# One kernel of two transformer blocks: where the second block's filters are made

## The chip, the cores and the metric

The kernel runs on one core of one Trainium2 chip. The time is the device time of one launch in microseconds (us); of several runs the median counts. Beside the timed runs there is one execution taken by the hardware profiler, from which all rows below come.

The engines are PE (matrix products), DVE and POOL (elementwise work), ACT (elementwise work and functions from tables; a table has to be loaded before its functions can run), and SP, which only issues transfers (DMA) here. Each engine works through its own list of instructions in order and waits for others at semaphores.

## The reference

Block 1 is two layers, each a mixer (a gated recurrence beside an attention) and a feed-forward part: in layer 0 a dense one, in layer 1 a mixture of 8 experts of which each token takes 2. A norm ends it. Block 2 is again two layers, conditioned by a vector, on 256 tokens and 256 tokens of context. The mixer of its layer 0 has a hyena branch, whose filters depend on nothing but weights:

```
def hyena_filters(n, w1, b1, w2, b2, freq, w3):
    hdn = jnp.sin(fr * (z @ w1 + b1))            # z: 256 x 33, positions
    hdn = jnp.sin(fr * (hdn @ w2 + b2))          # 64 wide
    filt = hdn @ w3                              # 2 orders x 2 directions x 512
    return filt.reshape(n, 2, 2, 512) * decay[:, None, None, :]

def bidir_long_conv(z, h_fwd, h_bwd, d_skip):
    taps = concatenate([h_fwd, 0, h_bwd[:0:-1]])                 # 512 long
    taps = taps * rsqrt(sum(taps * taps, axis=0) + EPS)
    y = irfft(rfft(z, 2 * n) * rfft(taps))[:n]
    return y + z * d_skip

def modulated_norm(x, g, shift, scale):
    return rms_norm_2(x, g) * (1 + scale) + shift
...
x = first_block(...)            # ends in rms_norm(x, final_norm)
h = modulated_norm(x, ...); h_ctx = modulated_norm(ctx, ...)
p = h @ w_in; p_ctx = h_ctx @ w_in
```

All is fp32. So between the experts of block 1 and the first product of block 2 stand two norms of x one behind the other, and one of the context.

## The kernel before

**Weights.** They stream through as 496 panels of 1 MB (128 x 2048 fp32) into a ring of six places in SBUF. SP issues panel p when panel p - 5 has been multiplied (`load`, line 466; the loop of line 479 for the first 462 panels, then one by one). Panels 0 to 461 belong to block 1; of them the experts have 8 x 42, three of which are a step. Then come 13 panels of block 2's layer 0 (`project2`, two of 512 columns in each), 4 of its output, and the same for layer 1.

**Products.** A product in fp32 is made of three products of a faster form: each operand is cut into a high part (ACT, the names with `high`, line 1425) and the rest (DVE subtracts the high part from the whole; `ring_low`, line 2709, for a panel of block 2, `h_parts`, line 2641, for the activations). 48 such products are a panel. Small things, the filters among them, are multiplied in plain fp32. All matrix products carry line 513 in the profile, all of ACT's operations line 1425.

**The end of the experts.** The rows of the last expert are put back to their tokens by products with a 0/1 matrix (`scatter`; `G`, `rows_high`, `rows_low`) into PSUM, and DVE adds them to x, a quarter at a time (line 2477).

**The seam.** `hyena_filters`, once per engine, holds the two norms and the filters interwoven, in the order in which it is written:

- PE: the first hidden product, the mean squares of x, the second hidden product, the mean squares of the context, taps(0) (the four products of order 0 with w3: two halves of the positions, `tb`, by two directions, `d`), the mean squares of x once more, taps(1), energy(0), spectrum(0) (eight products of 512 columns with the dft tables), energy(1). Then panels 0 and 1, then `spectrum(1)`, then panel 2.
- DVE: the halvings of panels 1 and 0, between them and after them the eight operations that bring each hidden layer's argument into the range of the sine (lines 2566 to 2573), the reciprocal of the first norm and eight scalings of x (line 2608), taps(0) and taps(1) times decay (line 2580), the reciprocal of the two second norms (line 2615), `condition(0)` (line 2634), and the loop of 16 steps that makes h (line 2620) and 16 that make its low part (line 2641). After the loop the reciprocals of the filters' energies (2587) and the eight operations that normalise the spectra (2596, 2599).
- ACT: squares, roots, the two sines, and the high parts (`y_parts`) of h. The sine and the root lie in different tables.
- POOL: for either order the sum and the difference of the two directions' taps (lines 1980 and 1981).
- SP: the filters' eight tables and the context, issued behind panels 463 (lines 488 to 492) and 466 (494 to 497).

**Block 1's start.** ACT squares x, PE sums it (8 products), ACT takes the root, DVE the reciprocal; panel 0 follows.

Of the kernel before, what the change touches and what calls it, by code (L numbers as in the profile page):

```python
# [126 lines left out]
def dft_tables():  # L127

    t = np.arange(S, dtype=np.float64)
    a = np.pi * np.outer(t, 2 * t + 1) / 512.0  # L130
    rows = lambda m: m.reshape(2, P, S).transpose(1, 0, 2).reshape(P, 2 * S)
    return np.concatenate([rows(np.cos(a)), rows(np.sin(a)), rows(np.cos(a).T / 256), rows(np.sin(a).T / 256)],
                          1).astype(np.float32)


def decay_table():
    t = np.linspace(0.0, 1.0, S, dtype=np.float32)[:, None]
    deltas = np.linspace(np.log(1e-2) / 1.5, np.log(1e-2) / 0.3, 512, dtype=np.float32)
    d = np.exp(-t * np.abs(deltas)).astype(np.float32)
    return d.reshape(2, P, 512).transpose(1, 0, 2).reshape(P, 1024)  # L140


def position_table():
# [3 lines left out]
    return np.concatenate([t, np.cos(f * w), -np.sin(f * w)], -1).T.astype(np.float32)  # L147


def two_blocks(nc, panels, x_in, ctx_in, consts_in, small_in, dft_in, decay_in, pos_in, w1_in, w2_in, w3_in,  # L150
               skip_in, rpb_in, out):
    stack = ExitStack()
    with stack:
# [40 lines left out]
        rt = sb("rt", 400)  # L194
        zrow = sb("zrow", 640, dt=BF16)
# [127 lines left out]
        COMBINED = (6144, 4096)  # L323

        def rnorm(o):

            return proj[:, 2304:2816] if o else proj[:, 3456:3968]

# [132 lines left out]
        def _(sp):  # L464
# [14 lines left out]
            with sp.Fori(1, looped) as r:  # L479
                for s in range(RING):  # L480
                    sp.wait_ge(DONE, r * RING + (s - RING + 1))
                    load(r * RING + s, s)
            biases = [(h, r) for h in range(8) for r in range(4)]
            for p in range(looped * RING, PANELS):
                sp.wait_ge(DONE, p - RING + 1)
                load(p, p % RING)
                if p == BLOCK1 + 1:
                    sp.dma_start(proj[0:33, 2816:2880], w1_in).then_inc(sem("filter_entry_landed"), 16)
                    sp.dma_start(proj[0:33, 2048:2304], pos_in).then_inc(sem("filter_entry_landed"), 16)
                    sp.dma_start(proj[0:64, 2880:2944], w2_in).then_inc(sem("filter_entry_landed"), 16)  # L490
                    sp.dma_start(proj[0:64, 0:2048], w3_in).then_inc(sem("filter_tables_landed"), 16)
                    sp.dma_start(cT[:, :], ctx_in).then_inc(sem("context_landed"), 16)
                elif p == BLOCK1 + 4:
                    sp.dma_start(proj[:, 8192:9216], decay_in).then_inc(sem("filter_tables_landed"), 16)
                    sp.dma_start(arena[:, 8704:9728], skip_in.partition_broadcast(P)) \
                      .then_inc(sem("filter_tables_landed"), 16)
                    sp.dma_start(arena[:, 4096:6144], dft_in).then_inc(sem("filter_tables_landed"), 16)
# [11 lines left out]
        def _(pe):  # L509
# [253 lines left out]

            def every_expert(p0):
# [45 lines left out]
                down(p0 + E * FFN - 1, 1, 0, STEPS)  # L810

# [152 lines left out]
            def compact_experts(p0):  # L964

                def scatter(ex, js):
                    for j in js:
                        if 4 * ex + j > 1:
# [110 lines left out]
                last_down()  # L1079
                pe.wait_ge(sem("rows_split"), E)  # L1080
# [3 lines left out]

            accs = [1]
            pe.wait_ge(sem("early_landed"), 32)
            pe.wait_ge(sem("accumulators_free"), 1)
            for layer in range(2):
                for j in range(4):
                    mean_square(j, MEAN_BANK[0])  # L1090
                if layer == 0:
                    pe.wait_ge(sem("consts_landed"), 16)
                    project1(layer)
# [15 lines left out]
            def hyena_filters():  # L1109
                h1 = proj[0:64, 2304:2560]  # L1110
                h2 = proj[0:64, 2560:2816]

                def taps(o):
                    for tb in range(2):
                        for d in range(2):
                            last = mm(bank(4 + tb * 2 + d), h2[:, tb * P:(tb + 1) * P],
                                      proj[0:64, (o * 2 + d) * 512:(o * 2 + d + 1) * 512], True, True)
                    last.then_inc(sem("filter_taps_sum"), 1)

                def energy(o):  # L1120
                    pe.wait_ge(sem("taps_squared"), nth(pe, "taps_squared"))
                    if o:
# [1882 lines left out]
```

## Time and profile before

| | us |
|---|---|
| median of 3 runs | 2281.84 |
| lowest and highest | 2280.45, 2283.21 |
| the profiled execution | 2276.82 |
| its span in the trace | 2275.0 |
| PE, DVE, ACT, POOL busy in the span | 2184.2, 1266.8, 690.9, 13.1 |
| 16 DMA engines, mean rate over the span | 234 GB/s |

The start of a row is counted from the start of the span. A row's duration is that of one instruction, or, with "x8" at its end, of eight behind one another; a plain fp32 product counts as two records. In square brackets stands how long the engine had been idle before, and what ended that.

### The profile page before, as it was taken

To read this page: it belongs to the slowest core of one execution; us is meant where nothing else is said; L and a number is where in the kernel's file an instruction comes from. 1 tells how busy PE (TensorE), PEld (TensorE's weight loads), DVE (VectorE), ACT (ScalarE), POOL (GpSimd) and SP (SyncE) were. 2 spreads that over 40 slices of the span, in tenths; PEclk is the share of its full clock that TensorE was granted. 3 is DMA by queue.
4 is the path that set the end of the run, shared out by engine and by line. 5 is a ranking of instruction groups with operands and counts; after the bars stand their busy time and mean duration, and the time that the engine had idled before them with its cause. 6 is when DMAs were issued, how large, how long until landed. Compare 5 with 4: busy or idle time off the path is not lost.

```text
span 2275.0 us, 41269 instructions
## 1 busy us (share of the span) xinstructions
PE 2184.2 (96%) x17170; PEld 1414.0 (62%) x17176; DVE 1266.8 (56%) x2570; ACT 690.9 (30%) x893; POOL 13.1 (1%) x25
## 2 busy tenths in 40 slices
PE   8999999999999899999999999999989999898988
PEld 7899899999899633333333333333336784677856
DVE  5765544437855344444444454445467666847783
ACT  6464433337464200010001000100024222634452
POOL 0000000000000000000000000000001000000000
PEclk9999999999999899999999999999999999999999
DMA  6244577756234299999999999999991220016400
GB/s 261 107 144 147 199 269 271 262 192 223 109 131 150 110 390 397 387 383 380 409 388 371 388 403 390 381 381 403 387 360 37 74 97 33 1 56 136 109 16 20
DMA packets 81811, 532.03 MB, mean 234 GB/s; under 512 B 16935, under 2 KB 17224, under 8 KB 17480
## 3 DMA queue, kind: packets, MB, share of 16 engines
q1 hardware_dynamic: 81528, 528.95, 61.0%
q8 instruction: 110, 1.80, 0.3%
q10 hardware_dynamic: 144, 1.05, 0.1%
q14 instruction: 29, 0.24, 0.0%
HBM read 528.91 MB, written 1.05 MB: 233 GB/s over the span
## 4 chain that ended last, share of the span: by engine, by line
PE 78%; DVE 12%; ACT 6%; issue 3%; DMA 1%; DVEq 0%; ACTq 0%; SPq 0%
PE ps L513 77%; ACT arena L1425 2%; ACT B_high L1425 1%; DMA ring<-panels 1%; PE ps L1343 1%; ACT L1425 1%; DVE arena L2822 1%; DVE arena L2184 1%; DVE arena L2208 1%; DVE ring_low L2709 1%; DVE arena L2198 1%; DVE ring_low L2070 1%; ACT P_high L1425 1%; DVE arena L2179 0%; DVE hT L2035 0%
## 5 line engine op out<-in xcount | busy, mean ns | idle before, releaser
L513 PE MATMUL ps<-ring,arena 128*32 128x512 f32 (+1 forms) x3056 | 894.0, 566 | 2.7 <-DMA ring<-panels 1.4
L513 PE MATMUL ps<-ring,hT 128*32 128x512 f32 x5376 | 794.9, 593 | 0.0
L513 PEld LDWEIGHTS ps<-ring,arena 128*32 128x32 f32 x3056 | 231.5, 110 | 593.7 <-issue 543.5
L1425 ACT ACTIVATE arena<-ps 96x256 f32<-96x256 f32 (+3 forms) x199 | 93.9, 478 | 883.8 <-PE ps L513 862.7
L2440 DVE STREAM_TRANSPOSE arena<-arena 32x64 f32<-32x64 f32 x1344 | 316.0, 235 | 20.9
L2487 DVE SCALAR_TENSOR_TENSOR arena<-arena,rt,ps 96x256 f32<-96x256 f32 x112 | 53.4, 477 | 472.4 <-ACT arena L1425 472.4
L513 PEld LDWEIGHTS ps<-ring,hT 128*32 128x32 f32 x5376 | 213.0, 110 | 6.9 <-issue 6.7
L513 PE MATMUL ps<-h_parts,ring_low 128*128 128x256 f32 x704 | 200.0, 284 | 0.0
L513 PE MATMUL ps<-h_parts,B_high 128*128 128x256 f32 x1024 | 189.3, 287 | 1.9 <-DVE h_parts L2044 1.1
L513 PE MATMUL ps<-y_parts,ring_low 128*128 128x256 f32 (+1 forms) x512 | 173.0, 338 | 0.0
L513 PEld LDWEIGHTS ps<-h_parts,B_high 128*128 128x128 f32 x1024 | 161.3, 194 | 3.2 <-issue 2.0
L2300 DVE TENSOR_TENSOR W_low<-ring,W_high 128x2048 fp32r<-128x2048 f32 x42 | 96.2, 2292 | 116.8 <-ACT W_high L1425 116.8
L513 PEld LDWEIGHTS ps<-h_parts,ring_low 128*128 128x128 f32 x704 | 135.9, 193 | 0.0
L513 PE MATMUL ps<-h_high,W_high 128*128 128x256 f32 x448 | 129.0, 288 | 2.8 <-DVE h_low L2049 1.7
L513 PE MATMUL ps<-h_low,W_high 128*128 128x256 f32 x448 | 126.6, 283 | 0.0
L513 PE MATMUL ps<-h_high,W_low 128*128 128x256 f32 x448 | 126.6, 283 | 0.0
L2070 DVE TENSOR_TENSOR ring_low<-ring,B_high 128x2048 fp32r<-128x2048 f32 x40 | 91.2, 2291 | 62.3 <-ACT B_high L1425 61.7
L1425 ACT ACTIVATE W_high<-ring 128x2048 fp32r<-128x2048 f32 x42 | 80.3, 1912 | 93.9 <-DMA ring<-panels 49.0
L513 PEld LDWEIGHTS ps<-y_parts,ring_low 128*128 128x128 f32 x512 | 98.1, 192 | 10.2
L1425 ACT ACTIVATE proj<-ps 128x512 f32<-128x512 f32 (+2 forms) x86 | 65.1, 756 | 104.5 <-PE ps L513 103.8
L513 PEld LDWEIGHTS ps<-h_high,W_high 128*128 128x128 f32 x448 | 85.7, 191 | 11.0 <-issue 9.2
L513 PEld LDWEIGHTS ps<-h_low,W_high 128*128 128x128 f32 x448 | 85.8, 191 | 0.0
(281 smaller groups left out, 3367.7 us busy)
## 6 DMA issues: line engine op xcount, KB each, us to landing
ring<-panels SPq DMA_DIRECT2D x496, 1024.0 KB, 7.3
arena<-rpb SPq DMA_DIRECT2D x32, 64.0 KB, 8.4
cst<-consts SPq DMA_DIRECT2D x1, 1632.0 KB, 12.1
xT<-x SPq DMA_DIRECT2D x1, 1024.0 KB, 4.8
cT<-ctx SPq DMA_DIRECT2D x1, 1024.0 KB, 13.6
arena<-dft SPq DMA_DIRECT2D x1, 1024.0 KB, 19.6
y<-xT ACTq DMA_DIRECT2D x1, 1024.0 KB, 3.9
proj<-w SPq DMA_DIRECT2D x1, 512.0 KB, 12.0
```

The costliest lines, as they stand in the source:

```text
L513: return nc.tensor.matmul(o, w, m, start=start, stop=stop, skip_group_check=skip)
L1343: last = nc.tensor.transpose(bank(TURN_BANKS[layer] + half)[:, c * P:(c + 1) * P], probs(layer, i, half)[:, c * P:(c + 1) * P], K(K_ID))
L1425: return nc.scalar.activation(o, i, fn, **kw)
L2070: V.tensor_tensor(wide_low(q, 0, PW), ring[:, (q % RING) * PW:(q % RING + 1) * PW], proj_high(layer, i).bitcast(F32), ALU.subtract).then_i ...
L2184: signal(V.tensor_tensor(v(E[lv % 2]), v(b), v(b)[:, :, B - 1:B].to_broadcast([P, 512 // B, 2 * B]), ALU.subtract), "level_exponent_ready")
L2198: signal(V.tensor_tensor(w(X), qk, w(E[lv % 2]), ALU.mult), "level_qk_ready")
L2208: step(V.reciprocal(lf, lf))
L2300: V.tensor_tensor(split(W_low, q, 0, PW), ring[:, (p % RING) * PW:(p % RING + 1) * PW], split(W_high, q, 0, PW).bitcast(F32), ALU.subtract ...
L2440: last = V.transpose(hidden_T(s)[group(b), :, 32 * g:32 * g + 32], src[group(g), :, b, :])
L2487: V.scalar_tensor_tensor(hb[s % 2], sg[s % 2], slot_weight[0:SLOTS, ex:ex + 1], bank(s % 2)[0:SLOTS, 256:512], ALU.mult, ALU.mult) \
L2709: V.tensor_tensor(wide_low(q, 0, PW), ring[:, (q % RING) * PW:(q % RING + 1) * PW], N_high[p % 2].bitcast(F32), ALU.subtract).then_inc(sem ...
L2822: signal(V.tensor_scalar(pr, pr, stat_of(3, i, half), None, ALU.mult), "probs_ready")
```

## The change

- **The hidden layers** (two products, 2 x 8 operations on DVE, two sines) are made at the start of block 1: the first ahead of its first norm, the second in the first panels of layer 0. Their result stays in a tensor of its own, `filter_hidden`. Their small weights come on ACT's queue at the start.
- **The tables** come while the experts run: SP issues w3 and the context after round 65 of the ring, decay after round 68, the dft tables after round 71, skip behind panel 468.
- **The last expert.** PE multiplies half of taps(0) (`half_taps(0, 1, 2)`) between the last expert's last panel and the scatter; ACT squares the context there. Each quarter of x is signalled alone (`x_part`).
- **The norms** (`final_norms`) hold no more of the filters than the two halves of taps(0).
- **Between the panels** of layer 0 `filter_step(turn)` makes the rest: after panel 0 taps(1), after 1 spectrum(0), after 2 both energies (one product each, since POOL adds the squares up first), after 3 and within 4 spectrum(1).
- **Radix 2.** Positions and frequencies are ordered even and odd, so that a spectrum needs four products instead of eight and a butterfly. ACT copies the products out, POOL normalises, adds skip and makes the butterfly: 18 operations in place of 4. The hyena's transposes and its last products read and write in that order, with a stride.
- No code of block 2's layer 1 is changed, nor of block 1 beyond the hidden layers.

The diff, cut to its core:

```diff
 # SP
-            with sp.Fori(1, looped) as r:
-                for s in range(RING):
-                    sp.wait_ge(DONE, r * RING + (s - RING + 1))
-                    load(r * RING + s, s)
+            rounds(1, 66)
+            sp.dma_start(proj[0:64, 0:2048], w3_in).then_inc(sem("filter_tables_landed"), 16)
+            sp.dma_start(cT[:, :], ctx_in).then_inc(sem("context_landed"), 16)
+            rounds(66, 69)
+            sp.dma_start(proj[:, 8192:9216], decay_in).then_inc(sem("filter_tables_landed"), 16)
+            rounds(69, 72)
+            sp.dma_start(arena[:, 4096:6144], dft_in).then_inc(sem("filter_inputs_landed"), 16)
+            rounds(72, looped)
...
 # PE
+            def half_taps(o, tb, b):
...
+                for d in range(2):
+                    last = mm(bank(b + d), filter_hidden[0:64, tb * P:(tb + 1) * P],
+                              proj[0:64, (o * 2 + d) * 512:(o * 2 + d + 1) * 512], True, True)
...
                 last_down()
+                pe.wait_ge(sem("rows_c_copied"), E)
+                half_taps(0, 1, 2)
                 pe.wait_ge(sem("rows_split"), E)
                 scatter(E - 1, (0, 1))
...
+            pe.wait_ge(sem("filter_inputs_landed"), 48)
+            mm(bank(3)[0:64, 0:S], W1_T, POS_T, True, True).then_inc(sem("filter_products_done"), 1)
...
+            def filter_step(turn, middle=False):
+
+                if turn == 0:
+                    pe.wait_ge(sem("taps_ready"), 1)
+                    half_taps(1, 0, 4)
+                    half_taps(1, 1, 6)
+                elif turn == 1:
+                    pe.wait_ge(sem("taps_ready"), 2)
+                    pe.wait_ge(sem("taps_combined"), 1)
+                    pe.wait_ge(sem("filter_inputs_landed"), 48 + 32)
+                    spectrum_half(0, 0, 4)
+                    spectrum_half(0, 1, 6)
+                elif turn == 2:
+                    pe.wait_ge(sem("spectrum_copied"), 2)
+                    for o in range(2):
+                        pe.wait_ge(sem("taps_summed"), o + 1)
+                        mm(bank(6 + o), K(K_ONE), rnorm(o), True, True).then_inc(sem("filter_products_done"), 1)
+                elif turn == 3:
+                    pe.wait_ge(sem("taps_root_ready"), 2)
+                    pe.wait_ge(sem("taps_combined"), 2)
+                    spectrum_half(1, 0, 6)
...
 # POOL
                 pool.tensor_tensor(hp, a[:, :, 0, :], a[:, :, 1, :], ALU.add)
                 pool.tensor_tensor(hm, a[:, :, 0, :], a[:, :, 1, :], ALU.subtract).then_inc(sem("taps_combined"), 1)
+                pool.wait_ge(sem("taps_squared"), o + 1)
...
+                step(pool.tensor_tensor(q[:, 0:1024], q[:, 0:1024], q[:, 1024:2048], ALU.add))
+                pool.tensor_tensor(rnorm(o), q[:, 0:512], q[:, 512:1024], ALU.add).then_inc(sem("taps_summed"), 1)
...
 # DVE
+            def final_norms():
+                dve.wait_ge(sem("filter_tables_landed"), 32)
+                taps_part(0, 1, 2)
+                condition(0)
                 root()
                 for k in range(KD):
...
-                taps(0)
-                taps(1)
                 dve.wait_ge(sem("root_ready"), nth(dve, "root_ready"))
-                step(V.reciprocal(rstd[:, :], rstd[:, :]))
-                condition(0)
-                dve.wait_ge(sem("context_landed"), 16)
+                step(V.reciprocal(rstd[:, S:512], rstd[:, S:512]))
+                root()
+                narrow_part(panel[0], 0)
                 for k in range(KD):
...
+                    if k == 3:
+                        taps_part(0, 0, 4)
+                        first_tap(0)
                 for s in range(2):
                     modulated_low(0, KD - 1, s)
-                taps_rnorm(0)
-                spectrum(0)
-                taps_rnorm(1)
-                return spectrum
+                narrow_part(panel[0], 1)
...
             def hyena_y(s):
...
-                signal(V.tensor_tensor(y3[:, 4:8, a], bank(4 * s, 2).rearrange("p (c n) -> p c n", c=4),
-                                       p2[:, :, a], ALU.mult), "hyena_y_done")
+                signal(V.tensor_tensor(y3[:, 4:8, a].rearrange(times, b=2),
+                                       bank(4 * s, 2).rearrange("p (c b t) -> p c b t", c=4, b=2),
+                                       p2[:, :, a].rearrange(times, b=2), ALU.mult), "hyena_y_done")
```

DVE's list from the last add to the first step of the loop, before the change (the two hidden layers are the runs from L2566 to L2573):

```order
L2477 TENSOR_TENSOR xT<-xT,ps 128x512 x4
L2550 UNCONDITIONAL_BRANCH
L2709 TENSOR_TENSOR ring_low<-ring,N_high_odd 128x2048
L2566 TENSOR_SCALAR proj<-ps,sml 64x256
...
L2573 TENSOR_SCALAR proj<-proj 64x256
L2029 RECIPROCAL rstd<-rstd 128x256
L2608 SCALAR_TENSOR_TENSOR xT<-xT,sml,rstd 128x256 x8
L2580 TENSOR_TENSOR proj<-ps,proj 128x1024 x2
L2583 MEMSET proj 1x512
L2580 TENSOR_TENSOR arena<-ps,proj 128x1024 x2
L2583 MEMSET arena 1x512
L2615 RECIPROCAL rstd<-rstd 128x512
```

And with the change (L2660 is half of taps(0), L2683 and L2704 are the loop's steps):

```order
L2575 TENSOR_TENSOR xT<-xT,ps 128x512 x4
L2651 UNCONDITIONAL_BRANCH
L2660 TENSOR_TENSOR proj<-ps,proj 128x1024
L2697 SCALAR_TENSOR_TENSOR ada_a<-ada,sml 128x16
L2110 RECIPROCAL rstd<-rstd 128x256
L2673 SCALAR_TENSOR_TENSOR xT<-xT,sml,rstd 128x256 x8
L2678 RECIPROCAL rstd<-rstd 128x256
L2110 RECIPROCAL rstd<-rstd 128x256
L2778 TENSOR_TENSOR ring_low<-ring,N_high_even 128x2048
L2683 SCALAR_TENSOR_TENSOR hT<-xT,ada_a,rstd 128x256
...
L2660 TENSOR_TENSOR proj<-ps,proj 128x1024
L2665 MEMSET proj 1x512
```

Both hidden layers, taps(1) and one halving have left this list; the other half of taps(0) and its memset, which releases POOL, stand inside the loop.

PE's list at the same place, from the scatter to panel 0, before:

```order
L513 MATMUL ps<-proj 64x256
L513 MATMUL ps<-hT,cst 128x256 x8
L513 MATMUL ps<-proj 64x256
L513 MATMUL ps<-hT,cst 128x256 x8
L513 MATMUL ps<-proj 128x512 x4
L513 MATMUL ps<-hT,cst 128x256 x8
L513 MATMUL ps<-proj 128x512 x4
L513 MATMUL ps<-proj,cst 128x512 x4
L513 MATMUL ps<-proj,arena 128x512 x8
L513 MATMUL ps<-proj,cst 128x512 x4
```

and with the change:

```order
L537 MATMUL ps<-G,rows_low 128x256
L1151 UNCONDITIONAL_BRANCH
L537 MATMUL ps<-hT,cst 128x256 x24
L537 MATMUL ps<-proj,filter_hidden 128x512 x2
L537 MATMUL ps<-y_parts,N_high_even 128x512
```

The mean squares stay; of the filters' 22 small products there only half of taps(0) is left.

## Rows read from the trace of the kernel before

**Rows 1.** The page, the chain that ended last: its share of the span by engine.

```profile
PE 78%; DVE 12%; ACT 6%; issue 3%; DMA 1%; DVEq 0%; ACTq 0%; SPq 0%
```

**Rows 2.** A piece of the chain inside the experts: start us, us, what.

```profile
1547.90 7.70 DMA ring<-panels
```

**Rows 3.** Timeline of PE around the seam: start us, us, instruction.

```profile
1719.62 7.03 PE L513 MATMUL ps<-proj,arena 128*128 128x512 f32 x16
1726.49 3.60 PE L513 MATMUL ps<-proj,cst 128*128 128x512 f32 x8
1729.52 0.79 PE L513 MATMUL ps<-y_parts,N_high_even 128*128 128x512 f32 x1
...
1740.85 0.39 PE L513 MATMUL ps<-y_parts,N_high_odd 128*128 128x512 f32 x1
...
1751.73 7.03 PE L513 MATMUL ps<-proj,arena 128*128 128x512 f32 x16
```

**Rows 4.** Timeline of DVE around the seam.

```profile
1690.26 1.28 DVE L2477 TENSOR_TENSOR xT<-xT,ps 128x512 f32<-128x512 f32 x2 [0.30 <-PE ps L513]
1692.17 2.29 DVE L2709 TENSOR_TENSOR ring_low<-ring,N_high_odd 128x2048 fp32r<-128x2048 f32 x1 [0.62 <-DVE xT L2477]
...
1702.98 1.75 DVE L2029 RECIPROCAL rstd<-rstd 128x256 f32<-128x256 f32 x1
1704.77 3.63 DVE L2608 SCALAR_TENSOR_TENSOR xT<-xT,sml,rstd 128x256 f32<-128x256 f32 x8
1708.97 2.48 DVE L2580 TENSOR_TENSOR proj<-ps,proj 128x1024 f32<-128x1024 f32 x2 [0.57 <-DVE xT L2608]
...
1719.41 3.35 DVE L2615 RECIPROCAL rstd<-rstd 128x512 f32<-128x512 f32 x1
1722.80 1.36 DVE L2634 SCALAR_TENSOR_TENSOR ada_a<-ada,sml 128x16 f32<-128x16 f32 x1
...
1735.68 1.27 DVE L2641 SCALAR_TENSOR_TENSOR h_parts<-hT,ada,y_parts 128x256 fp32r<-128x256 f32 x3
```

**Rows 5.** Timeline of ACT in the seam.

```profile
1691.82 2.19 ACT L1425 ACTIVATE hT<-xT 128x512 f32<-128x512 f32 x4 [2.11 <-DVEq L2024]
...
1697.57 0.42 ACT L1425 ACTIVATE proj<-proj 64x256 f32<-64x256 f32 x1 [1.76 <-DVE proj L2573]
...
1699.80 1.28 ACT L1425 ACT_TABLE_LOAD   x1
1701.10 0.47 ACT L1425 ACTIVATE rstd<-ps,cst 128x256 f32<-128x256 f32 x1
```

**Rows 6.** Timeline of POOL in the seam, and all executions of DVE's line 2634.

```profile
1719.46 2.36 POOL L1980 TENSOR_TENSOR proj<-arena 128x1024 f32<-128x1024 f32 x1 [2.61 <-DVE arena L2583]
1721.78 2.35 POOL L1981 TENSOR_TENSOR proj<-arena 128x1024 f32<-128x1024 f32 x1
...
L2634 DVE SCALAR_TENSOR_TENSOR ada_a<-ada,sml x2: 168/762/1357, 1722.8 to 2006.5; 128x16 f32<-128x16 f32 x2
```

**Rows 7.** Stretches of the experts: five engines' busy time; last PE's clock, DMA share, GB/s.

```profile
1504.00:1590.00 86.00, 85.45 (x792) 28.06 (x786) 41.55 (x150) 6.21 (x13) 0.00 (x0) 1.00 1.00 401
1594.00:1598.00 4.00, 4.00 (x44) 1.22 (x40) 2.87 (x9) 0.00 (x0) 0.00 (x0) 1.00 0.80 336
1598.00:1602.00 4.00, 4.00 (x44) 1.25 (x40) 0.76 (x3) 0.38 (x1) 0.00 (x0) 1.00 0.86 309
1602.00:1606.00 4.00, 4.00 (x40) 1.13 (x36) 2.54 (x11) 0.00 (x0) 0.00 (x0) 1.00 1.01 416
```

**Rows 8.** Timeline of PE at the start of block 1.

```profile
6.34 6.11 PE L513 MATMUL ps<-arena,cst 128*128 128x256 f32 x16 [6.34 <-DMA sml<-small]
```

**Rows 9.** Block 2, layer 0: DVE and ACT between panels; all executions of line 2791.

```profile
1771.71 2.29 DVE L2709 TENSOR_TENSOR ring_low<-ring,N_high_even 128x2048 fp32r<-128x2048 f32 x1 [8.60 <-ACT N_high_even L1425]
...
1843.52 1.00 ACT L1425 ACTIVATE proj<-ps 128x1024 f32<-128x1024 f32 x1
...
L2791 DVE TENSOR_TENSOR yT<-ps,proj x2: 1224/1224/1225, 1942.5 to 1950.8; 128x1024 f32<-128x1024 f32 x2
```

More of the change, by code:

```diff
@@ L1171, in project2, with spectrum_half @@
-            def project2(layer, filter_spectrum=None):
+            def spectrum_half(o, cs, b):
+                for tb in range(2):
+                    last = mm(bank(b + tb), arena[:, 4096 + cs * 512 + tb * S:][:, 0:P],
+                              proj[:, COMBINED[o] + cs * 1024 + tb * 512:][:, 0:512], True, True)
+                last.then_inc(sem("filter_products_done"), 1)
+            def filter_step(turn, middle=False):
[18 more added lines that the diff above has]
+                    spectrum_half(1, 0, 6)
+                elif middle:
+                    pe.wait_ge(sem("spectrum_copied"), 3)
+                    spectrum_half(1, 1, 6)
+                else:
+                    pe.wait_ge(sem("spectrum_copied"), 4)
@@ L1172, in project2 @@
+            def project2(layer):
                 chunks = qk_chunks(layer)
@@ L1223, in project2 @@
                         last.then_inc(DONE, 1)
+                        if layer == 0:
+                            filter_step(turn)
                         continue
-                    if layer == 0 and p == 2:
-                        filter_spectrum(1)
                     if layer == 1 and p == 2:
@@ L1235, in project2 @@
                         for m in range(2):
+                            if layer == 0 and turn == 4 and m:
+                                filter_step(turn, True)
                             for k in range(KD):
@@ L1239, in project2 @@
                     last.then_inc(DONE, 1)
+                    if layer == 0 and turn <= 4:
+                        filter_step(turn)
                     for i in range(len(chunks)):
@@ L1857, in project2 @@
                 for turn in range(IN2):
+                    if layer == 0 and turn == 4:
+                        spectrum_copy(1, 1, 6)
                     multiplied(1)
@@ L1860, in project2 @@
                         pair_copy(layer, p0, turn)
+                    if layer == 0 and turn == 1:
+                        taps_square(1)
+                        spectrum_copy(0, 0, 4)
+                        spectrum_copy(0, 1, 6)
+                    elif layer == 0 and turn == 2:
+                        taps_root(0)
+                        taps_root(1)
+                    elif layer == 0 and turn == 3:
+                        spectrum_copy(1, 0, 6)
                     for c in range(len(chunks)):
@@ L2096, in project1 @@
                         proj_part(layer, p0, IN1 + 2)
+                    if layer == 0 and i == 1:
+                        filter_phase(1)
                     if i == 2:
@@ L2545, in every_expert @@
                 weigh(E - 1)
+                for j in range(4):
+                    dve.sem_inc(sem("x_part"), 1)
             many = dve.value_load(crowded[0:1, 0:1], min_val=0, max_val=1)
@@ L2676, in project2 @@
                             qk_norm(chunks, i)
+                    if layer == 0 and p == 2:
+                        dve.wait_ge(sem("taps_root_ready"), 2)
+                        for o in range(2):
+                            signal(V.reciprocal(rnorm(o), rnorm(o)), "rnorm_ready")
                     if layer == 1 and 9 <= p < 13:
```

330 lines of the change are left out of this document (160 added, 170 removed).

## The prediction

> **What bounds the kernel now.** I read the page's chain of waits first, then the timelines of the engines around the place where block 1 ends and block 2 begins (the seam), then the busy time of the DMA engines by stretch. The chain is 78% matrix products [rows 1]; transfers are 1% of it, yet inside the experts it does hang for 7.70 us on the landing of panels [rows 2]. So two places matter: the seam, where PE waits or does work of the filters, and the experts, where the transfers are just as late as PE.
>
> In the seam PE has no panel of weights to multiply from the last expert's end until 1729.52; panel 1 begins at 1740.85, and before panel 2 stand the eight fp32 products of spectrum(1), from 1751.73 [rows 3]. What PE waits for is DVE: the last add of the experts' rows begins at 1690.26 and ends, 1.28 later, at 1691.54; then come two halvings (2.29 each), twice the eight operations of a hidden layer, a reciprocal, eight scalings, taps(0), taps(1) and a reciprocal; only then the loop that makes h and its low halves, from 1724.16 to 1736.95 [rows 4].
>
> **The change, the seam.** I lay out a new schedule from the rows' durations, as if nobody disturbed anybody.
> - Scatter: two fp32 products of half_taps stand before it on PE. Eight of 512 columns take 1726.49 - 1719.62 = 6.87 [rows 3], 0.86 each. PE had waited there, so of their 1.7 only about 0.4 shows: last add ends 1691.9.
> - The squares start after each add instead of after all four. Before, they took 2.19 from 1691.82 [rows 5]; now the last is over 0.65 (a quarter of 2.19, and its start) after the last add, 1692.55. A table load of 1.28 [rows 5], the root 0.47 and its start [rows 5]: 1694.5. DVE's reciprocal of 256 columns 1.75 [rows 4]: 1696.3.
> - Eight scalings 3.63 [rows 4]: 1699.9; the context's reciprocal 1.75: 1701.7. The last square ends 1700.6, its products 1701.4, the root 1701.9, the second reciprocal 1703.7, the halving of panel 0 2.29 [rows 4]: 1706.0.
> - The loop. In the trace its 29 single steps and the triple lie between 1724.16 and 1735.68, a pitch of 0.40 [rows 4]; 32 steps are 12.7. One half of taps(0) now stands in its middle with its memset: half of 2.48 [rows 4] and 0.65, 1.9 in all. Last low half 1720.6. PE, free from long before, runs at DVE's pace and ends panel 0 1.4 later (six products of the last step): 1722.0. Before it was 1740.85. **-18.9.**
> - Given back between the panels: half_taps(1) before panel 1, four products, +3.4; before panel 2 four of spectrum(0) where eight of spectrum(1) stood, -3.4; the energies, one product each, before panel 3, +1.7; spectrum(1) in twos before panels 4 and 5, +3.4. Changing between fp32 and panel products costs a little each time (the first panel product has 0.79 instead of 0.39 [rows 3]), +0.4 in all. **Seam: -18.9 + 3.4 - 3.4 + 1.7 + 3.4 + 0.4 = -13.4.**
>
> **The lock.** That schedule has a flaw. POOL's sum and difference of taps(0) (2.36 and 2.35 each [rows 6]) become ready in the middle of DVE's loop. In the trace one small DVE operation with two inputs in SBUF, 128x16, took 1357 ns at 1722.80 and 168 ns later in the run [rows 6]; it ended at 1724.16, and POOL's operation of 1721.78 ended at 1724.13 [rows 6]. It had been held until POOL was done. The reciprocal before it, one input, ran beside POOL at its full pace. The steps of the loop read two SBUF tensors, so I let both POOL operations hold them in full: **+4.7**. In the old kernel the same two stood before the loop, where DVE had little to do.
>
> The Trainium skill, page "SBUF — State Buffer", section "Who interferes with whom", calls it an exclusive lock between DVE and GpSimd, and says that a DVE instruction with two SBUF inputs contends with a GpSimd instruction that reads SBUF; by that rule, the trace agrees. It speaks against this change; were the two engines to share without holding each other, the seam would be worth -13.4, with the lock it is -8.7.
>
> **The transfers.** w3 (0.52 MB), the context (1.05), the decay (0.52) and the dft tables (1.05), 3.15 MB, leave the stretch after the last experts' panels, where PE had no panel to wait for, and are queued on SP between expert panels of rounds 66 to 72 of the ring, about 1500 to 1590. There the 16 DMA engines are busy to 1.00 at 401 GB/s [rows 7]. Whatever is put in pushes all later panels back; PE can take that only from its own lead. At 416 GB/s, the rate of a nearby stretch [rows 7], 3.15 MB take 7.6. Behind them the DMA engines were idle for (0.20 + 0.14) x 4 = 1.4 [rows 7], which absorbs as much, and I put 0.6 more on the lead that the ring can give up, an estimate: PE hangs on a landing in the chain only at single places [rows 2]. **+5.6**; bounds 0 (the ring's lead covers all) and 7.9 (401 GB/s, nothing absorbed). SP itself loses nothing: four issues of half a microsecond beside panels that are issued five ahead.
>
> **Block 1.** The first hidden product stands before PE's mean squares (6.11 from 6.34 [rows 8]) and waits for three small transfers: 0 to +1.0, I take 0.4. The second sine (0.42 [rows 5]) stands in a chain of ACT that the next matrix work awaits: +0.3. DVE's phase operations are 2 x 8 small ones of some 0.3 beside PE's panels, nothing. Sum **+0.7**, bounds 0 and 2.
>
> **Hyena.** Its last products now read PSUM and write with a stride. Before they took 1224 ns twice [rows 9], both on the path to the output projection. If a strided element costs as much as a packed one: 0; if double: +2.4. No row shows such a stride in fp32; with nothing that points to a doubling I stand nearer to no cost, **+0.5**.
>
> The same skill page, section "Door 1: The DMA port swizzle", says that non-contiguous access of PSUM slows matmuls and that four-byte elements may be a few apart in SBUF for free; it would put the sum near the upper end, +2.4, and no row here shows it.
>
> **Sum.** -13.4 + 4.7 + 5.6 + 0.7 + 0.5 = **-1.9 us**. The profiled execution took 2276.82 (its span 2275.0), 5 under the median of 2281.84. I put the difference on the median: 2281.84 - 1.9 = **2280.0**. The chip's answer is readable to about 0.2%, 4.6 us, so this forecast is "no change".
>
> **Rivals.**
> - A (forecast): POOL's two operations hold the loop, the transfers cost. Bounds: the lock 2.4 (one of the two falls between DVE steps) to 4.7, transfers 3.5 to 7.9, the rest -0.5 to +2. 2276 to 2284. **0.47.**
> - B: no lock in the loop, because POOL starts late or alternates with DVE's short steps: -1.9 - 4.7 = -6.6, **2275.2**. For it: DVE is steadily busy, so POOL may get the port only at gaps. Against it: the 1357 ns. **0.24.**
> - D: the transfers are absorbed. -1.9 - 5.6 = -7.5, **2274.3**. For it: the chain has just a few pieces on DMA. Against it: share 1.00 over 86 us. **0.12.**
> - C, the slower side: POOL's later work holds DVE where DVE is what PE waits for. POOL now also normalises and combines both spectra: per order three operations of 1024 and three of 512 elements, by [rows 6] 3 x 2.36 + 3 x 1.2 = 10.7, in all 21.4, over panels 3 to 6, where each low half of a panel is a DVE operation with two SBUF inputs that PE needs before it may begin. DVE idled 8.60 before one of these [rows 9]; what exceeds it is paid: 21.4 - 8.6 = 12.8, and two more reciprocals (3.35 each) lie in the same place. -1.9 + 12.8 = +10.9, **2292.7**. It decides if POOL gets the port nearly without pause; the low halves are three or four in that stretch, and each would have to wait its turn several times, which is why it gets only **0.10.** The added waits of ACT's copies of panels 6 and 8 for these spectra cost nothing: the copy of panel 8 began at 1843.52 [rows 9], 1830 after the change, and even with 21.4 of POOL's work laid end to end behind panel 4 (about 1785) it is done before.
> - E: several bounds at their dear ends (strided reads double, transfers 7.9, block 1 +2), +3.6, or the moved work simply gives back in one place what it saves in another: 2280 to 2288. **0.07**, half of it slower.
>
> **How the numbers follow.** Faster by over 0.2% (under 2277.3): B, D and the cheapest tenth of A: 0.24 + 0.12 + 0.04 = 0.40. Slower (over 2286.4): C, half of E, 0.13. Between: 0.47. The range reaches from B and D with 3 us for their unknown terms, 2271.5, to the dear end of A and E, 2286. Left out are C and the case that both B and D hold (2269.6).
>
> **What would show each step.** In the timeline of DVE after the seam: the loop's steps at 0.40 with two holes of about 2.35 beside POOL's two operations (A), or none (B). The loop's end near 1720.6 + 4.7, shifted by what came before. In the experts: the start of the last expert's last step some 5.6 later than in the trace of before, with PE idle on landings from about 1500 on (A), or at the same time (D). In panels 3 to 6: DVE's halvings at 2.29 (A) or at 4 and more beside POOL, with PE idle on ring_low (C). In the hyena: the two last operations at 1.22 or at 2.4. The prediction falls if the roots wait for something that I have not put in the schedule, or if the ring had more lead than the landings show.

## The result: 0.27% slower

| | before | changed |
|---|---|---|
| median, 10 runs each (us) | 2282.3 | 2287.07 |
| lowest to highest | 2278.69 to 2285.43 | 2281.38 to 2291.83 |
| ratio, 95% interval | | 1.0027 (1.0017 to 1.0037) |
| profiled execution, its span | 2276.82, 2275.0 | 2285.83, 2284.0 |

A forecast of 2280.0, a range up to 2286, and a likeliest case of "no change": all missed, the range by 1.1 us. The spans differ by 9.0 us, the medians by 4.8; the profiled execution of before was one of the short ones (5.5 under its median), that of after lies 1.2 under its own. So some 4 us of the 9 belong to the two executions.

**Where the time is.** I went through both traces in order and subtracted the starts of the same piece of work. ACT's first operation in each step of the experts (96x256) is a good landmark, as there are 112 of them:

| piece of work | before | after | difference |
|---|---|---|---|
| third expert step | 798.91 | 800.04 | +1.1 |
| 90th expert step | 1504.13 | 1508.26 | +4.1 |
| 112th, the last | 1678.74 | 1691.48 | +12.7 |
| last add of the experts' rows ends | 1691.54 | 1705.09 | +13.6 |
| panel 0 ends | 1740.85 | 1743.48 | +2.6 |
| panel 2 begins | 1758.19 | 1761.19 | +3.0 |
| panel 5 begins | 1796.09 | 1804.22 | +8.1 |
| end of the span | 2275.0 | 2284.0 | +9.0 |

In the page's chain that ended last the transfers had 1%, now they have 4% (it answers [rows 1]). That share is no measure of the loss: it stays at 3 to 4% in all versions below from which the tables have left the experts and in which the loss is gone.

```profile
PE 75%; DVE 12%; ACT 6%; DMA 4%; issue 3%; ACTq 0%; DVEq 0%; SPq 0%
```

**The experts.** Two pieces of that chain (start, us, what; they answer [rows 2]), then SP's issue of the tables, and ACT's two steps behind it with the idle time before each:

```profile
1504.92 11.89 DMA ring<-panels
1557.74 9.90 DMA ring<-panels
```

```profile
1498.26 0.56 SPq L508 DMA_DIRECT2D proj<-w  x1
1498.88 0.87 SPq L509 DMA_DIRECT2D cT<-ctx  x1
```

```profile
1508.26 0.38 ACT L1454 ACTIVATE arena<-ps 96x256 f32<-96x256 f32 x1 [7.35 <-PE ps L537]
1522.44 0.38 ACT L1454 ACTIVATE arena<-ps 96x256 f32<-96x256 f32 x1 [13.79 <-PE ps L537]
```

The step took 14.18 us; the usual one is 7.73. A panel issued at 1504.92 was 11.89 us under way. What the transfers did meanwhile, by stretch (the columns are those of [rows 7]):

```profile
1502.00:1504.00 2.00, 2.00 (x24) 0.65 (x20) 1.89 (x9) 0.00 (x0) 0.00 (x0) 1.00 0.99 418
1504.00:1506.00 2.00, 2.00 (x24) 0.61 (x20) 0.42 (x2) 0.00 (x0) 0.00 (x0) 1.00 1.11 242
1506.00:1508.00 2.00, 2.00 (x24) 0.52 (x16) 0.00 (x0) 0.00 (x0) 0.00 (x0) 1.00 0.97 217
1508.00:1510.00 2.00, 2.00 (x24) 0.65 (x20) 1.25 (x5) 0.38 (x1) 0.00 (x0) 1.00 0.98 393
```

All 16 engines are busy, and yet the rate is halved for four us. w3 is on its way then (issued at 1498.26): 0.52 MB to 64 partitions. The other tables go to 128. In the four us some 0.9 MB were moved (242 and 217 GB/s), more than w3 has, so the panels beside it were slow too.

**The seam.** DVE's loop and POOL beside it (they answer [rows 4] and [rows 6]):

```profile
1727.17 0.48 DVE L2665 MEMSET proj<- 1x512 f32 x1 [0.16 <-DVE proj L2660]
1727.69 2.69 DVE L2683 SCALAR_TENSOR_TENSOR hT<-xT,ada_a,rstd 128x256 f32<-128x256 f32 x1
1730.30 2.56 DVE L2704 SCALAR_TENSOR_TENSOR h_parts<-hT,ada,y_parts 128x256 fp32r<-128x256 f32 x1
1732.78 0.47 DVE L2683 SCALAR_TENSOR_TENSOR hT<-cT,ada_a,rstd 128x256 f32<-128x256 f32 x1
```

```profile
1727.74 2.36 POOL L2039 TENSOR_TENSOR proj<-proj 128x1024 f32<-128x1024 f32 x1 [1726.37 <-DVE proj L2665]
1730.06 2.52 POOL L2040 TENSOR_TENSOR proj<-proj 128x1024 f32<-128x1024 f32 x1
```

Two steps of the loop, 0.48 elsewhere, take 2.69 and 2.56, each about as long as the POOL operation beside it. PE behind them (the answer to [rows 3]), and its granted clock, the third number from the right:

```profile
1722.85 0.77 PE L537 MATMUL ps<-y_parts,N_high_even 128*128 128x512 f32 x1 [5.30 <-DVE h_parts L2704]
...
1733.71 0.80 PE L537 MATMUL ps<-y_parts,N_high_even 128*128 128x512 f32 x1 [5.07 <-DVE h_parts L2704]
1734.30 0.63 PE L537 MATMUL ps<-h_parts,N_high_even 128*128 128x512 f32 x1
```

```profile
1722.00:1724.00 2.00, 1.15 (x3) 0.98 (x4) 2.00 (x6) 1.16 (x4) 0.00 (x0) 0.50 0.04 8
1726.00:1728.00 2.00, 2.00 (x10) 1.64 (x9) 1.80 (x3) 0.02 (x1) 0.26 (x1) 1.00 0.00 0
1734.00:1736.00 2.00, 2.00 (x5) 1.54 (x5) 2.00 (x7) 1.35 (x3) 0.00 (x0) 0.50 0.00 0
```

PE stood idle for 5.30 us ahead of panel 0 and for 5.07 in its middle. Behind each pause it went on at clock 0.50 (1.2 GHz instead of 2.4) before it came back to 1.00: a product begins every 0.43 us instead of every 0.23.

### The profile page after: what moved, and what is told of

Read it like the earlier page. It is cut to its first block, busy times and chain, and to the rows that moved or that the text cites. A ratio compares the mean times of both kernels' runs of the same rounds, so it can differ in the third digit from the quotient of the medians.

```text
span 2284.0 us, 41224 instructions
## 1 busy us (share of the span) xinstructions
PE 2177.2 (95%) x17142; PEld 1411.1 (62%) x17148; DVE 1270.9 (56%) x2559; ACT 691.8 (30%) x896; POOL 50.6 (2%) x41
## 3 DMA queue, kind: packets, MB, share of 16 engines
HBM read 528.91 MB, written 1.05 MB: 232 GB/s over the span
## 4 chain that ended last, share of the span: by engine, by line
PE 75%; DVE 12%; ACT 6%; DMA 4%; issue 3%; ACTq 0%; DVEq 0%; SPq 0%
PE ps L537 73%; DMA ring<-panels 4%; ACT arena L1454 2%; ACT B_high L1454 2%; PE ps L1372 1%; DVE arena L2267 1%; DVE arena L2894 1%; ACT L1454 1%; DVE ring_low L2151 1%; DVE arena L2291 1%; ACT P_high L1454 1%; DVE arena L2281 0%; DVE arena L2262 0%; DVE rstd L2110 0%; DVE hT L2116 0%
## 5 line engine op out<-in xcount | busy, mean ns | idle before, releaser
L537 PE MATMUL ps<-h_parts,B_high 128*128 128x256 f32 x1024 | 188.7, 286 | 3.0 <-DVE h_parts L2125 2.2
L537 PE MATMUL ps<-y_parts,N_high_even 128*128 128x512 f32 (+1 forms) x208 | 78.3, 377 | 16.2 <-DVE h_parts L2704 14.6
```

The lines of the kernel that those rows point to most:

```text
L537: return nc.tensor.matmul(o, w, m, start=start, stop=stop, skip_group_check=skip)
```

## The experiments

All medians are against the kernel before on the same chip; a kernel with one run has no interval. For the seam I use one landmark, the end of the last add, and give from there, in us of each profiled execution:

| kernel | panel 0 begins | last low half ends | panel 0 ends | panel 2 begins |
|---|---|---|---|---|
| before | 38.0 | 45.4 | 49.3 | 66.7 |
| changed | 17.8 | 34.1 | 38.4 | 56.1 |
| changed, again | 17.8 | 34.1 | 37.3 | 55.0 |
| POOL late | 17.8 | 29.8 | 32.1 | 49.8 |
| tables late | 17.8 | 34.1 | 37.3 | 55.0 |
| both | 17.8 | 29.8 | 32.0 | 49.7 |
| changed, hole filled | 17.8 | 34.1 | 36.3 | 54.0 |
| both, start filled | 17.8 | 29.8 | 32.1 | 49.8 |
| both, start filled, taps behind the loop | 17.8 | 27.9 | 30.1 | 47.9 |
| the same, not filled | 17.8 | 27.9 | 31.6 | 49.3 |

For the experts I use the time from the 89th step to the 112th, "the stretch": 182.3 in before (1496.40 to 1678.74), 190.9 in the changed kernel, and 182.3 to 183.7 in the six profiled executions of the kernels below that have no table in it. "The control" is the changed kernel, run again.

### The changed kernel again

> The changed kernel itself, as a control on the same chip as the three that follow. Expected by all theories: a ratio of 1.002 to 1.004 to the kernel before, and the last low half of the loop about 34 us after the last add of the experts' rows.

2285.68 (8 runs), ratio 1.0018 (1.0007 to 1.0030). The stretch took 190.2; the step with w3 and the context 15.3. Panel 0 ended 1.1 us sooner behind the last add than in the first trace, with 8 slow products behind the hole in place of 13.

### POOL late

```diff
+        WIDE_IN_BLOCK1 = max(v for (e, n), v in seen.items() if n == "wide_panel_split") - 2 * IN2
...
                 pool.wait_ge(sem("taps_ready"), o + 1)
+                if o == 0:
+                    pool.wait_ge(sem("wide_panel_split"), WIDE_IN_BLOCK1 + 2)   # panel 1 halved
```

> The changed kernel, with one edit: POOL's sum and difference of taps(0) wait until DVE has halved panel 1, that is until the loop is over. Theory (lock and clock): the two held steps of the loop (2.69 and 2.56 instead of 0.48) go, 4.5 us, and with them the hole of 5.07 us in PE's work, after which PE ran at clock 0.50 until 1739.4 and ended panel 0 2.9 us later than DVE's last step allows; panel 0 ends 7.3 us earlier against the last add, the kernel is 7 us faster than the changed one. Rival (lock alone): PE's clock falls anyway in this loop, 4.5 us. Rival (no effect): the loop was paced by ACT's high parts, 0.

2281.51 (12 runs), ratio 1.0000 (0.9990 to 1.0010). The loop's two long steps are gone, the last low half comes 4.3 us sooner, and panel 0 ends 5.2 sooner than in the control (6.3 than in the first trace). In the traces that is more than the lock alone, and less than the 7.3 that I expected; in medians it is 4.2. The tables were still among the expert panels here, and the stretch took 190.5, the step with w3 and the context 16.1. The last low half of this kernel is followed by 2.2 us of products, not by the 1.4 that I had worked out.

### Tables late

```diff
-            rounds(1, 66)
+            rounds(1, looped)
             sp.dma_start(proj[0:64, 0:2048], w3_in).then_inc(sem("filter_tables_landed"), 16)
             sp.dma_start(cT[:, :], ctx_in).then_inc(sem("context_landed"), 16)
-            rounds(66, 69)
             sp.dma_start(proj[:, 8192:9216], decay_in).then_inc(sem("filter_tables_landed"), 16)
-            rounds(69, 72)
-            sp.dma_start(arena[:, 4096:6144], dft_in).then_inc(sem("filter_inputs_landed"), 16)
-            rounds(72, looped)
...
                 load(p, p % RING)
+                if p == BLOCK1 + 2:
+                    sp.dma_start(arena[:, 4096:6144], dft_in).then_inc(sem("filter_inputs_landed"), 16)
```

> The changed kernel, with one edit: w3, the context and the decay are issued right behind the last expert's last panel, the dft tables behind panel 464, instead of between the expert panels of rounds 66 to 72. Theory (every inserted byte is paid): the expert steps lose their one-time delays of 6.1, 0.3 to 1.9 and about 0.6 us, and the kernel is 8 us faster than the changed one. Rival (the delays were chance drift of the transfers, and only the profiled run had them): no difference. Rival (moved wait): the tables land too late for the last expert's half of taps(0) and the seam gives 2 to 5 us back; the step that would show it is DVE's first operation after the last add.

2278.18 (12 runs), ratio 0.9997 (0.9988 to 1.0006), 7.5 under the control. The stretch took 182.35, as in before; nothing came back in the seam, where every landmark is that of the control. So the delay was not chance, and the tables are in time when they are issued behind the last expert panel.

### Both

> Both edits together. If they are independent, 7.3 + 8 = 15 us faster than the changed kernel, about 10 faster than the kernel before (ratio 0.9955). If lock alone: 12. If the transfers' part is chance: 7.

2272.79 (5 runs), ratio 0.9964 (0.9951 to 0.9977). 12.9 under the control, against 7.5 and 4.2 apart: within the noise they add up.

### The context and w3 apart, in the kernel before

```diff
...
+            rounds(1, 66)
+            sp.dma_start(cT[:, :], ctx_in).then_inc(sem("context_landed"), 16)
+            rounds(66, 72)
+            sp.dma_start(proj[0:64, 0:2048], w3_in).then_inc(sem("filter_tables_landed"), 16)
+            rounds(72, looped)
...
-                    sp.dma_start(proj[0:64, 0:2048], w3_in).then_inc(sem("filter_tables_landed"), 16)
-                    sp.dma_start(cT[:, :], ctx_in).then_inc(sem("context_landed"), 16)
```

> The kernel before, with only two transfers moved into the experts: the context (1.05 MB, 128 partitions) behind round 65 and w3 (0.52 MB, 64 partitions) behind round 71. Theory (every byte is paid, at the rate at which it moves): the expert step that receives the context grows by about 2.6 us over its 7.7 (1.05 MB at 401 GB/s); w3, which moved at about 210 GB/s in the changed kernel, costs as much again, 2.5, though it is half the bytes; together 5.1 between the steps at 1500 and at 1671. Rival (bytes alone count): 2.6 and 1.3, together 3.9. Rival (the ring absorbs them): under 1.

One run, 2284.22. SP issued the context at 1498.57 and w3 at 1591.44. ACT's steps behind either:

```profile
1508.56 0.38 ACT L1431 ACTIVATE arena<-ps 96x256 f32<-96x256 f32 x1 [7.35 <-PE ps L519]
...
1604.02 0.38 ACT L1431 ACTIVATE arena<-ps 96x256 f32<-96x256 f32 x1 [8.62 <-PE ps L519]
1614.50 0.38 ACT L1431 ACTIVATE arena<-ps 96x256 f32<-96x256 f32 x1 [10.10 <-PE ps L519]
```

The context, 1.05 MB, cost nothing: eight steps in a row of 7.7 us. w3, half as large, lengthened its step to 10.5. The stretch took 184.3. With this run "every byte is paid" is refuted: the ring has a lead after all, at least as long as the context's 2.6 us, and w3 is worse than its bytes.

### The hole filled

```diff
                         for k in range(KD):
+                            if layer == 0 and k == 3:
+                                for _ in range(20):
+                                    mm(bank(3), zrow[:, 0:P], zrow[:, P:640], True, True)
                             pe.wait_ge(sem("h_mod_split"), nth(pe, "h_mod_split", 2 - layer))
```

> The changed kernel, with 20 bf16 products of a zero tile into an unused bank put before panel 0's fourth step, where PE otherwise stands idle for 5.07 us while POOL holds DVE. Nothing else changes; the two held steps of the loop stay at 2.7 and 2.6. Theory (the hole costs the clock): PE's clock stays at 1.00 behind the hole, no product of 0.63 us after it, and panel 0 ends 1.4 to 2.5 us after the last low half instead of 3.1 to 4.3. Rival (panel 0's slow products have another cause, the lock itself): the slow products behind the hole stay.

One run, 2287.71. DVE's two steps stayed at 2.69 and 2.57. PE's timeline:

```profile
1731.69 4.49 PE L537 MATMUL ps<-zrow 128*128 128x512 bf16 x20
1736.94 0.50 PE L537 MATMUL ps<-y_parts,N_high_even 128*128 128x512 f32 x1 [0.76 <-DVE h_parts L2707]
1737.27 0.40 PE L537 MATMUL ps<-h_parts,N_high_even 128*128 128x512 f32 x1
```

No slow product follows, and panel 0 ends 2.2 us after the last low half instead of 3.1 (control) and 4.3 (first trace). So PE's pause cost the clock, and the clock 0.9 to 2.1 us. (The time as a whole is long since the step with w3 took 17.4 here.)

### The start filled

The version with both edits, and 22 such products ahead of panel 0.

> The version with both edits (POOL late, tables behind the last expert panel), and 22 such products of a zero tile on PE ahead of panel 0, where it is idle for 5.30 us. Theory (clock): the 9 to 11 products of 0.63 us at panel 0's beginning go; since DVE paces the loop (1.58 us a step against PE's 1.36), only what PE is behind at the loop's end comes back, 0.5 to 1 us: panel 0 ends 1.4 us after the last low half instead of 2.2. Rival: the clock falls whatever PE multiplies, 0; or the products delay panel 0, up to 1 us slower.

2272.13 (8 runs), ratio 0.9967 (0.9956 to 0.9978). PE no longer had a pause of 5.30 us nor one slow product, and panel 0 ended at 32.1, as without. The clock that came back was worth nothing: PE waited for DVE all the same.

### Taps behind the loop

The last version, with one edit more:

```diff
-                    if k == 3:
-                        taps_part(0, 0, 4)
-                        first_tap(0)
                 for s in range(2):
                     modulated_low(0, KD - 1, s)
+                taps_part(0, 0, 4)
+                first_tap(0)
                 narrow_part(panel[0], 1)
```

> As the last, and the half of taps(0) with its memset (1.9 us of DVE) moved from the middle of the loop to behind it, ahead of panel 1's halving. Theory: the last low half comes 1.9 us earlier, PE then waits about 0.5 for the taps before panel 1: 1 to 1.9 us faster than the last kernel, panel 1 begins 1.4 earlier. Rival: PE's own pace (1.36 a step) becomes the bound, as DVE's pause was where it caught up: 0 to 0.5.

2269.55 (6 runs), ratio 0.9956 (0.9943 to 0.9969). The last low half, panel 0's end and panel 2's start are all 1.9 us sooner.

### w3 alone late, and the context alone late

The changed kernel, with the one line of w3, or of the context, behind `rounds(72, looped)`.

> The changed kernel, with w3 alone (0.52 MB, 64 partitions) moved behind the last expert panel; the context, the decay and the dft tables stay between the expert panels. Theory (w3's form): the context alone fits into the ring's lead, as it did in the previous run, where its expert step stayed at 7.7 us; the step of 14.2 to 17.4 us that receives both in the changed kernel falls to 7.7 to 9, and the kernel is 6 to 8 us faster than the changed one, though 2.6 of 3.15 MB stay where they are. Rival (bytes): w3 is a sixth of them, the step falls by 1.3, the kernel by as much. Rival (sum of the two transfers over the lead): it falls by 2.5 to 4, and about 4 stay.

2281.24 (10 runs), ratio 1.0001 (0.9992 to 1.0011). The context went out at 1500.46 among the expert panels; ACT's steps around it, and the rate of a stretch that read 218 in the changed kernel (1505 to 1508):

```profile
1502.73 0.38 ACT L1454 ACTIVATE arena<-ps 96x256 f32<-96x256 f32 x1 [7.34 <-PE ps L537]
1510.46 0.38 ACT L1454 ACTIVATE arena<-ps 96x256 f32<-96x256 f32 x1 [7.35 <-PE ps L537]
1518.18 0.38 ACT L1454 ACTIVATE arena<-ps 96x256 f32<-96x256 f32 x1 [7.35 <-PE ps L537]
```

```profile
1505.00:1508.00 3.00, 3.00 (x32) 0.87 (x28) 1.55 (x7) 0.00 (x0) 0.00 (x0) 1.00 1.02 429
```

The stretch took 182.3, that of before, with 2.6 of the 3.15 MB still in it. With w3 away, the whole loss in the experts was gone. The decay is the nearest comparison that the runs have, as many bytes as w3 but over 128 partitions; issued at 1546.81, it did not lower the rate:

```profile
1552.00:1554.00 2.00, 2.00 (x24) 0.48 (x17) 0.94 (x4) 0.00 (x0) 0.00 (x0) 1.00 0.97 397
1554.00:1556.00 2.00, 2.00 (x24) 0.78 (x20) 0.00 (x0) 0.00 (x0) 0.00 (x0) 1.00 1.08 434
```

The median gained 4.4 on the control, less than the stretch's 7.9. It was measured on another chip, and in the profiled execution most of the difference lies at the other end. From the last add to panel 12 this kernel keeps the control's times. Its remaining work, which is the same code in all versions, took 403.4 us, and 399.7 in the version "tables late":

```profile
1874.30:2274.00 399.70, 359.70 (x2137) 273.73 (x2135) 261.35 (x508) 177.61 (x332) 2.96 (x16) 0.99 0.20 53
1875.10:2278.50 403.40, 363.56 (x2137) 276.80 (x2136) 261.37 (x508) 177.11 (x332) 2.94 (x16) 0.97 0.20 53
```

DVE and ACT were busy as long as there. PE had a mean granted clock of 0.97 instead of 0.99 and was busy for 3.9 us more. The clock falls in some places of block 2 in one execution and not in the next, and that moves a single execution by up to 4 us.

> The changed kernel, with the context alone (1.05 MB, 128 partitions) moved behind the last expert panel; w3, the decay and the dft tables stay. Theory (w3's form): the step that receives w3 alone stays at 10 to 11 us, 2.8 over its 7.7, as in the run with w3 behind round 71. Rival (bytes): it falls by 2.6 from 14.2 to 17.4. Rival (only both together exceed the lead): 7.7.

One run, 2284.52. The step with w3 alone took 11.0; but the steps behind it, with the decay and the dft tables, lost more than in any other kernel (8.8, 8.7, 8.6), and the stretch came to 188.7. This kernel has 2.1 MB of tables among the expert panels, less than the 2.6 of the one before, and lost 6.4 us where that one lost nothing, so neither the bytes nor their sum over the lead explains it. It looks as if w3 spends the lead, and what comes behind it is then paid; that is my reading of one execution.

### With and without the filling

> The fastest version so far again, as a partner of the next on the same chip. Expected ratio to the kernel before 0.9956, and 30.1 us from the last add to panel 0's end.

2271.73 (5 runs), ratio 0.9958 (0.9945 to 0.9972); the landmarks of its first run to 0.03.

> The same version without the 22 products of a zero tile ahead of panel 0. With the pause in DVE's loop gone, PE has nowhere to catch up what the 9 to 11 slow products at the start of panel 0 cost it (0.2 us each). Theory (the clock costs where PE can't catch up): panel 0 ends 0.5 to 2 us later than with the products, 31 to 32 us after the last add. Rival (PE catches up against DVE's 1.58 a step in any case, as in the earlier pair, where the products gained nothing): 30.1, the same time.

2269.92 (5 runs), ratio 0.9952 (0.9938 to 0.9965). Panel 0's first products:

```profile
1714.10 0.77 PE L535 MATMUL ps<-y_parts,N_high_even 128*128 128x512 f32 x1 [5.31 <-DVE h_parts L2705]
1714.66 0.63 PE L535 MATMUL ps<-h_parts,N_high_even 128*128 128x512 f32 x1
```

Panel 0 ended at 31.6 instead of 30.1: with no pause left in DVE's loop the slow start does cost 1.4 us in the trace. In the medians of five runs it can't be seen; the two intervals overlap almost wholly. These two are the fastest versions, 0.42 to 0.48% under the kernel before. None of the changed kernel's work is left out of them; what they save is waiting.

## Why the prediction was wrong, step by step

Two terms of the sum failed, and a third was too small. The transfers were to cost 5.6 us, by their bytes, and cost 7.9 to 8.6, nearly all of it through w3. The seam was to gain 8.7 and gained 4.6 (5.7 in the second execution), since the new schedule was too short and no term stood for PE's clock. Block 1 was to cost 0.7 and cost some 2.3 in the mean of twelve executions. The mechanism of case A, POOL holding DVE's loop, was right.

- **Rows read.** The two places, the seam and the experts' transfers, were the right ones. What lies between them moves from one execution to the next: the experts from the third step to the 90th took 705.2 us in before and 706.1 to 711.5 in the other kernels, none of which changes anything there.
- **The new schedule of the seam.** The loop began 15.2 us behind the last add, not 14.1: the first root waited 0.53 for PE's eight mean squares, which can't start before the scatter's last product and take 3.5; I had let them end with the squares. The loop itself took 14.7 without the lock; I had 14.6. The scatter cost 0.8, not 0.4. Behind the last low half PE needs 2.2, not 1.4.
- **The lock.** Right: 4.7 expected, 4.3 measured as the difference with and without POOL's two operations beside the loop. Its place and size were read from one DVE operation of 1357 ns, which is little to go by.
- **What the lock brings with it.** Missed. A term stood nowhere for PE's clock, though the hole of 5.07 us followed from the schedule. It was worth 0.9 to 2.1 us. The Trainium skill, page "SBUF — State Buffer", section "Who interferes with whom", says that PE never waits on anyone. That holds for its access to SBUF; by a semaphore it waited here for an engine that was locked out, and paid twice, with the pause and with the clock behind it.
- **Given back between the panels.** Panel 2 to panel 5: +5.1, as worked out; the first two terms cancelled to 0.4. POOL's work on the spectra did hold DVE (halvings of 3.76 and 4.37 instead of 2.29), but PE waited for none: no pause of 0.25 us or more stands between its products there. Case C was real as a mechanism and free.
- **The seam in sum.** -8.7 forecast; -4.6 from the last expert step to panel 5 in the first trace, -5.7 in the second.
- **The transfers.** The mis-sized term, and the wrong reason. 5.6 forecast, 7.9 to 8.6 measured (11.3 in one run). It lies at or above my upper bound, which was built from bytes and a rate. I took the DMA share of 1.00 to mean that nearly every byte is paid, and put the ring's lead at 0.6 us. The runs show that 2.6 MB cost nothing, case D, and that the loss came and went with w3, 0.52 MB in 64 partitions. There was slack in spite of the share: a step of 7.73 us takes in three panels, 3.15 MB, that is 407 GB/s, and stretches of the same queue read 416 to 434. By these numbers a step makes up for 0.2 to 0.5 us, an estimate. The size of w3 was in the diff, and so was its form. The same page of the Trainium skill, section "Door 1: The DMA port swizzle", says that a transfer over 64 partitions is no faster than one over 32; I read that section for strides and passed over this. The trace shows half the rate while w3 is on its way, 217 against 418 GB/s; no run here has a transfer over 32. Half rate alone makes w3 cost 2.5; that the step lost 6.5 to 9.7, and that w3 lost 2.8 and 3.3 without the context behind it, though the lead can take 2.6, is not explained by it.
- **Block 1.** 0.7 forecast, with bounds 0 and 2; +1.1 at the experts' start in the first trace. That trace is one of the short ones: in the twelve executions with this edit the third expert step began at 799.9 to 803.3, 801.3 in the mean, and at 798.9 and 799.2 in the two without it. So the cost is nearer to 2.3. Part of it is that PE's mean squares began at 8.26 instead of 6.34; where the rest lies was not followed up.
- **Hyena.** DVE's last products took 1225 ns, as before (1224): no cost, so the dear end of +2.4 did not come. What was said of them ahead of the result was half wrong: by the code they read PSUM with a stride (neighbours stand 128 elements apart), but write SBUF packed. PE's transposes, to which I gave nothing, cost 0.1 in each of four groups, 0.4 in sum. 0.5 was forecast; from panel 5 to the end the first trace had 0.9 us more than before, the second 0.9 less, so the sum of this part is not resolved.

In sum: -1.9 forecast, +4.8 measured in the medians. By the traces the transfers are 2.3 to 3.0 of the difference of 6.7, the seam 3.0 to 4.1, and block 1 some 1.6. Each of these shares comes from single executions and can be off by 1 us.

**Open.** Why one narrow transfer costs three times its own length when the context stands right behind it was not settled. Nor was w3 tried in 128 partitions, as PE reads it from 64. So that it is w3 is shown; that it is its 64 partitions is argued, from the decay, which has the same bytes over 128 and cost nothing.

## What to carry to other kernels

Ask of a transfer that moves into a saturated stretch not only how many bytes it has but over how many partitions it runs: here the full-width ones vanished in the ring's lead, and the narrow one ate it. Where POOL reads SBUF beside a loop of DVE operations with two SBUF inputs, count nearly its whole length on the loop (here 4.3 of 4.9 us), and then ask what PE's pause does to PE's clock. Release such helper work with a semaphore behind the loop, not at the moment when its data is ready. And look at more than one execution before you give a few us of a long trace to the change.

## What the runs showed of the hardware that I had not expected

- While a transfer of 0.52 MB over 64 partitions was on its way, 16 busy engines moved 217 to 242 GB/s; with one of 1.05 MB over 128 in the same queue they moved 429, and with one of 0.52 MB over 128 partitions 397 and 434.
- PE was granted 0.50 behind pauses of 5.07 and 5.30 us and kept it for 7 to 13 products; 20 products of a zero tile in the pause kept it at 1.00.
- From panel 5 to the end, the same code took 477.8 to 481.8 us in the twelve executions of the changed kernel and its versions. DVE and ACT were busy equally long in the two compared above; PE's mean granted clock differed.
- Loading a stationary tile whose fp32 elements stand two apart took 209 ns (the middle number, the median), packed, in the kernel before, 141:

```profile
L1293 PEld LDWEIGHTS ps<-cst,proj x32: 194/209/222, 1895.0 to 1900.2; 128*128 128x128 f32 x32
```

- Reading PSUM with a stride of 128 elements did not lengthen DVE's product of 128x1024, 1224 before:

```profile
L2862 DVE TENSOR_TENSOR yT<-ps,proj x2: 1225/1225/1225, 1951.0 to 1959.3; 128x1024 f32<-128x1024 f32 x2
```
